# Two transformer blocks in one launch: a rearranged key-norm preparation, a recurrence whose triangular inverse runs in crossed halves with predicated copies, and a final norm inside the last stage

## The chip, the cores and the metric

One core of a Trainium2 chip runs the whole program in one launch. The metric is the device time of one execution in microseconds (us). A time is given as the median of several executions; a profiled execution is a run of its own, with its own time.

## The reference

The program computes two blocks, one after the other, on 256 tokens of width 1024, all in float32.

First block: a layer norm, then a projection `h @ w_in` that feeds two groups. One is latent attention with 8 heads. The other is a recurrence (RWKV-7) with 8 heads of 64 x 64 state. Then an output projection, a layer norm, 32 experts of which each token takes 4, and a second layer norm. The modulation vectors come from `ada_w` (1024 x 6144), which the program reads in three thirds. The recurrence, cut to its core, with the normalised key `kk`:

```
kk = k_h * k_k;  kk = kk / max(norm(kk), 1e-12)
k_h = k_h * (1 + (a_h - 1) * k_a)
sa    = state @ (-kk_t)
state = state * w_t + sa (x) (kk_t * a_t) + v_t (x) k_t
out_t = state @ r_t
o = (groupnorm(out) * gn_g + gn_b + bonus) * g
```

Second block: two layers, each a feed-forward net of width 2816, a mixing part with three kinds of attention, and a second feed-forward net; then the final norm:

```
return x * rsqrt(mean(x * x) + 1e-6) * final_norm
```

## The kernel before, in words

**Form.** Every engine has its own list of instructions, and semaphores order them across engines. The program is cut into stages (`Stage`); between two stages there is a barrier of all engines, in the profile a wait for `L221`. The activations are kept with features on partitions (`xT`, `hT`: 128 x 8 x 256). Within a stage the order is written out by hand.

**Weights.** SP issues the loads of 1 MB and 2 MB into a ring of 12 slots; a load waits until the slot's last user has told `used`. In the expert stage two rings are loaded for 32 experts, one after another. The first 8 MB for the experts are asked for in the recurrence stage (L1032 to L1035), further ones from the stage behind it and from L1486 on.

**Attention stage (L706 to L824).** TensorE goes through 8 heads: scores of head h + 2, values of head h - 1, transposes of head h (`turn`), and in `aside(h)` one unit of the second third of the modulation sums (`sum_ada`, L291). VectorE does mask, maximum, scaling; ACT the exponentials and copies. At the end ACT takes the root of the key norms (L799) and copies the modulation rows (L801).

**Preparation stage (L858 to L984).** SP loads the constants (`rc`, L870), the first output rows and eight units of `ada_w`. VectorE takes maximum and reciprocal of the key norm (L951, L952) and then a masked running sum of the decays (L957, `tensor_tensor_scan`), whose mask `no_start` comes with the constants. Behind it are the factors alpha, beta, kappa, rho (L970 to L976). TensorE spreads the key norm, makes gate, bonus and the transposes of the factors, which ACT copies to `nat`.

**Recurrence stage (L993 to L1335).** The 256 tokens are 4 chunks of 64. There are 16 systems (head half, head pair, token half) with two chunks each, one on partitions 0 to 63 and one on 64 to 127. For each the inverse of a unit lower triangular 64 x 64 matrix is grown by doubling blocks, in 5 levels (`LEVELS`, L1086). A level has, for two groups q of 8 systems: POOL masks the level's part out of the lower matrix (L1044); TensorE multiplies it with the transposed inverse (x, L1096); ACT copies the result (L1233); TensorE makes the growth of the transposed inverse (L1064) and of the inverse (L1071); VectorE adds both (L1294, L1297). Both products of a system stay on their own rows and columns of the array, so that a pair of chunks uses two of its four quarters of 64 x 64. Before the levels are the products of beta and kappa with alpha and rho (L1056) and the lower product (L1081), and VectorE's masks (L1272 to L1288). Behind them are a2v (L1113), za (L1124, L1127), ta (L1135), the chunk transition M (L1146, L1151), the inputs N (L1159, L1164), three steps over the chunks with the last third of the modulation sums between them, and the outputs.

A float32 matmul is executed in two passes. The profile has a record for each pass, and one for its weight load.

**Last stages.** The feed-forward nets split each weight into two parts of fewer bits and do three passes (`L2243`, `L2258`), with VectorE and ACT making the parts. Behind the last one VectorE adds the sums to `xT` (L2221). The final norm is a stage of its own (L2951 to L2995): squares of all columns, one sum over partitions by a product with ones (L2962), root, reciprocal, eight scalings (L2987), 16 transposes (L2968), four copies (L2979) and four stores.

## Time and profile before

| what | value |
|---|---|
| median of 3 runs | 2345.15 us |
| lowest and highest | 2336.08 and 2348.59 us |
| the profiled execution, its own time | 2340.77 us |
| its span in the profile | 2339.0 us |
| its mean granted TensorE clock | 0.974 |
| TensorE busy | 2184.0 us, 93% |
| VectorE busy | 1086.6 us, 46% |
| ACT busy | 698.2 us, 30% |
| POOL busy | 16.9 us, 1% |
| DMA | 626.63 MB, mean 268 GB/s |

A busy share is an average over stages with different limits, so the table alone does not say what bounds a stage. A row of the timeline has the start in us, the duration in us, engine and line, what is written and what is read, how many instructions are merged, and in brackets how long the engine had been idle and who ended it. A row of the windows has the stretch, its length, and for each engine the busy time and the number of instructions, then the granted TensorE clock as a share of 2.4 GHz, the mean share of the DMA engines and what they moved in GB/s.

### The profile page before, as it was taken

What the parts mean: (1) busy time and instruction counts of PE and PEld (TensorE: products, weight loads), DVE (VectorE), ACT (ScalarE), POOL (GpSimd) and SP (SyncE); (2) the same over time, 40 slices, a digit from 0 to 9 for tenths busy, and PEclk for the clock granted to TensorE, in tenths of its full rate; (3) what the DMA queues carried; (4) which work ended last, traced back from release to release, by engine and by line L of the source; (5) the groups of instructions that cost most, each with busy time, mean ns of one, the idle gap of its engine ahead of it and who ended that gap; (6) DMA issues with size and microseconds to landing.
All of it is one profiled execution on the core that took longest, in us unless ns stands there. A gap on an engine that the chain in (4) does not pass through costs nothing. (4 is left out here: it accounts for less than half of the span.)

```text
span 2339.0 us, 37294 instructions
## 1 busy us (share of the span) xinstructions
PE 2184.0 (93%) x15721; PEld 1593.4 (68%) x15721; DVE 1086.6 (46%) x1686; ACT 698.2 (30%) x884; POOL 16.9 (1%) x16
## 2 busy tenths in 40 slices
PE   6979799999999999999989999999999999999998
PEld 5757544433333333333439999879999999889997
DVE  4774511211111111111127557777566556777554
ACT  3542311111111111111115335345334334445332
POOL 0011000000000000000000000000000000000000
PEclk8989999999999999999989999999999999999999
DMA  9343789999999999999966564325555655434651
GB/s 379 138 178 148 285 344 430 430 430 430 430 430 430 430 430 430 430 430 430 414 248 198 180 192 150 109 91 193 186 181 162 198 187 173 126 100 135 199 182 52
DMA packets 200079, 626.63 MB, mean 268 GB/s; under 512 B 13160, under 2 KB 149928, under 8 KB 164136
## 3 DMA queue, kind: packets, MB, share of 16 engines
q1 hardware_dynamic: 197368, 623.41, 69.0%
q10 hardware_dynamic: 2608, 1.72, 0.3%
q8 instruction: 80, 1.31, 0.2%
q14 instruction: 23, 0.19, 0.0%
HBM read 624.05 MB, written 1.05 MB: 267 GB/s over the span
## 5 line engine op out<-in xcount | busy, mean ns | idle before, releaser
L2009 DVE TENSOR_TENSOR w_low<-ring,w_high 128x2048 fp32r<-128x2048 f32 x168 | 383.9, 2290 | 265.7 <-ACT w_high L2004 265.7
L2004 ACT ACTIVATE w_high<-ring 128x2048 fp32r<-128x2048 f32 x168 | 319.9, 1909 | 273.3 <-PE bank L2243 140.8
L1762 PE MATMUL bank<-ring,ut 128*64 128x512 f32 x1024 | 244.3, 624 | 40.6 <-DMA ring<-in_exp_w_dram 40.5
L1734 PE MATMUL bank<-ring,xt 128*64 128x512 f32 x1024 | 223.3, 594 | 0.3 <-ACT xt L1816 0.3
L1734 PE MATMUL bank<-ring_odd,xt 128*64 128x512 f32 x1024 | 223.3, 594 | 0.0
L1762 PEld LDWEIGHTS bank<-ring,ut 128*64 128x64 f32 x1024 | 71.2, 142 | 198.0 <-issue 123.2
L2258 PE MATMUL bank<-h_high,w_high 128*128 128x256 f32 x1408 | 187.3, 281 | 6.5 <-ACT h_high L2149 3.6
L2258 PE MATMUL bank<-h_high,w_low 128*128 128x256 f32 x1408 | 186.2, 281 | 1.4 <-DVE w_low L2009 1.4
L2258 PE MATMUL bank<-h_low,w_high 128*128 128x256 f32 x1408 | 186.1, 281 | 1.3 <-DVE h_low L2188 1.3
L1820 ACT ACTIVATE sg<-glu 128x512 f32<-128x512 f32 x32 | 20.2, 630 | 542.6 <-DVE glu L1883 542.6
L2258 PEld LDWEIGHTS bank<-h_high,w_high 128*128 128x128 f32 x1408 | 176.1, 189 | 7.6 <-ACT h_high L2149 4.3
L2258 PEld LDWEIGHTS bank<-h_high,w_low 128*128 128x128 f32 x1408 | 175.4, 189 | 1.7 <-DVE w_low L2009 1.7
L2258 PEld LDWEIGHTS bank<-h_low,w_high 128*128 128x128 f32 x1408 | 175.3, 189 | 1.5 <-DVE h_low L2188 1.5
L1899 DVE SCALAR_TENSOR_TENSOR xT<-bank,mod,xT 128x256 f32<-128x256 f32 x128 | 55.6, 480 | 247.4 <-PE bank L1776 247.4
L1734 PEld LDWEIGHTS bank<-ring,xt 128*64 128x64 f32 x1024 | 72.3, 137 | 143.1 <-issue 143.1
L1734 PEld LDWEIGHTS bank<-ring_odd,xt 128*64 128x64 f32 x1024 | 72.2, 137 | 142.9 <-issue 142.9
L1882 DVE TENSOR_SCALAR lin<-bank 128x256 f32<-128x256 f32 x64 | 26.7, 417 | 257.6 <-PE bank L1734 257.6
L1875 DVE TENSOR_SCALAR choose<-base 128x128 fp32r<-128x128 f32 x32 | 9.1, 287 | 236.0 <-PE bank L1762 236.0
L1833 ACT ACTIVATE y<-bank 64x512 f32<-64x512 f32 x64 | 37.9, 592 | 259.5 <-PE bank L1762 258.7
L2243 PE MATMUL bank<-u_high,w_low 128*128 128x256 f32 x704 | 92.0, 279 | 0.0
L2243 PE MATMUL bank<-u_low,w_high 128*128 128x256 f32 x704 | 91.9, 279 | 0.0
L2243 PE MATMUL bank<-u_high,w_high 128*128 128x256 f32 x704 | 91.9, 279 | 0.0
(544 smaller groups left out, 2813.4 us busy)
## 6 DMA issues: line engine op xcount, KB each, us to landing
ring<-in_exp_w_dram SPq DMA_DIRECT2D x64, 2048.0 KB, 27.2
ring_odd<-in_exp_w_dram SPq DMA_DIRECT2D x64, 2048.0 KB, 28.4
ring<-in_exp_w_dram SPq DMA_DIRECT2D x128, 1024.0 KB, 25.6
ring<-in_ffn_w_gate_dram SPq DMA_DIRECT2D x44, 1024.0 KB, 5.4
ring<-in_ffn_w_up_dram SPq DMA_DIRECT2D x44, 1024.0 KB, 5.4
ring<-in_ffn_w_down_dram SPq DMA_DIRECT2D x44, 1024.0 KB, 4.9
ring<-in_w_in_dram SPq DMA_DIRECT2D x36, 1024.0 KB, 5.4
ring<-in_ada_w_dram SPq DMA_DIRECT2D x24, 1024.0 KB, 12.7
```

Of the source, the lines that this page charges most:

```text
L1734: ins = nc.tensor.matmul(bank[b][at:at + SLOTS, :], xt[:, c, SLOTS * side:SLOTS * side + SLOTS], (ring, ring_odd)[side][:, c, 512 * q:512 ...
L1762: ins = nc.tensor.matmul(bank[2 + dh][64 * dh:64 * dh + 64, :], ut[:, r % 4, 64 * (r // 4):64 * (r // 4) + 64], w[:, x, 512 * dh:512 * dh ...
L1820: nc.scalar.activation(sg[:, :], glu[:, :], ACT.Sigmoid, scale=SW_ALPHA).then_inc(sem("sg_ready"), 1)
L1833: nc.scalar.activation(y[64 * side:64 * side + 64, 512 * dh:512 * dh + 512], bank[2 + dh][64 * dh:64 * dh + 64, :], ACT.Copy).then_inc(sem ...
L1875: nc.vector.tensor_scalar(choose[:, side, :], const("half_of"), const("expert_of")[:, bass.ds(e, 1)], None, ALU.mult).then_inc(sem("chosen ...
L1882: nc.vector.tensor_scalar(lin[:, 256 * b:256 * b + 256], pairs[:, :, 1], LIMIT, -LIMIT, ALU.min, ALU.max)
L1899: ins = nc.vector.scalar_tensor_tensor(xT[:, m, :], bank[6 + n % 2][:, T * j:T * j + T], mod[:, 40 + m:41 + m], xT[:, m, :], ALU.mult, ALU ...
L2004: nc.scalar.activation(w_bufs[0][u % BUFS], ring2[:, u % RING2, :], ACT.Copy).then_inc(high2, 1)
L2009: nc.vector.tensor_tensor(w_bufs[1][u % BUFS], ring2[:, u % RING2, :], w_bufs[0][u % BUFS].bitcast(F32), ALU.subtract).then_inc(low2, 1)
L2243: ins = nc.tensor.matmul(sums(m // 2)[:, T * (m % 2):T * (m % 2) + T], w[:, at:at + P], v[:, T * x:T * x + T], start=(g == 0 and k == 0 an ...
L2258: ins = nc.tensor.matmul(b[:, T * x:T * x + T], w[:, at:at + P], h[:, c, :], start=(k == 0 and x == 0 and c == 0), stop=(k == 2 and c == D ...
```

## The change

In words, stage by stage:

- **Attention.** The eight units of modulation sums are added two at a time in `aside` of heads 0 to 3. The root of the key norm is taken behind the exponentials of the last head; maximum, reciprocal and the copy of the modulation rows go to VectorE, ahead of its last copy. ACT ends with a sigmoid of one column.
- **Preparation.** `no_start` is made with two memsets. The copies of `gate` on ACT go behind the exponentials. The transposes of the modulation rows go to another bank and right behind the key product. A second table, the block masks (12 x 64 bytes a partition), is loaded; the table of constants shrinks from 1728 to 192 columns.
- **Recurrence.** ACT sets `inv` and `inv_t` to the identity and copies the lower product unmasked. VectorE puts the first blocks in by `copy_predicated` with byte masks. The lower product is made a second time with its two factors' places on the rows crossed. The systems are in two groups, even and odd; the rows of the inverse of the even ones are exchanged. Growth of the transposed inverse of one group is put in turn with x of the other group. Each growth is put in by `copy_predicated` from a bank. POOL has no work. `a2v` lies beside `nat` (which grows by a fifth), and za is one product of 128 columns. ACT's clears go between its copies, VectorE's bonus and gate scaling behind za. The second load of output rows waits for `n_ready`.
- **Last stage.** The final norm is part of the last feed-forward stage. Transposes are products of `xT` with a diagonal of the gains; row sums are products of the squares with one column of ones; root and reciprocal are on two columns; the factor comes in with the last copies, half on ACT and half on VectorE.

The core of the diff:

```diff
@@ attention
-                    sum_ada(pe, 1, bank[6], range(h, h + 1))
+                    if h < 4:
+                        sum_ada(pe, 1, bank[6], range(2 * h, 2 * h + 2))
...
+                def key_inverse():
+                    dve.wait_ge(sem("key_root"), 1)
+                    st.step(nc.vector.tensor_scalar(key_norm, key_norm, 1e-12, None, ALU.max))
+                    nc.vector.reciprocal(key_norm, key_norm)
+                    dve.wait_ge(used, UNIT[("ada1", ADA_THIRD - 1)] + 1)
+                    nc.vector.tensor_copy(mod_rows[:, :], bank[6][:, :])
@@ preparation
-                dve.wait_ge(sem("const_loaded"), 16)
+                st.step(nc.vector.memset(no_start, 1.0))
+                st.step(nc.vector.memset(no_start[:, 0:HP * T:CH], 0.0))
                 dve.wait_ge(sem("acts_done"), 1)
...
                 dve.wait_ge(sem("factor_ready"), 1)
                 st.step(nc.vector.tensor_tensor(flat(k), flat(k), factor, ALU.mult))
+                dve.wait_ge(sem("mod_turned"), 1)
@@ recurrence
-                sp.wait_ge(sem("ta_ready"), 1)
+                sp.wait_ge(sem("n_ready"), 1)
                 load_unit(sp, "wo", 0, wo_rows(1), 2)
...
+            def inverse_rows(s_, ph):
+                return half_rows(ph if s_ % 2 else 1 - ph)
...
+                for n in range(LEVELS):
+                    wait_x(n, 1)
+                    wait_growth_t(n, 0)
+                    for s_ in range(0, NS, 2):
+                        for ph in range(2):
+                            grown = growth_t(s_, ph)
+                        for ph in range(2):
+                            ins = x_product(s_ + 1, ph)
+                    grown.then_inc(sem("growth_t0"), 1)
+                    ins.then_inc(sem("x_ready1"), 1)
+                    growth(n, 0)
+                    if n in KAPPA_LEVELS:
+                        pe.wait_ge(sem("products_taken"), 4 + 2 * n)
+                        products(kappa, n, lambda h2: 6 + h2)
...
-                            nc.tensor.matmul(bank[s_ // 4][r, at:at + 64], inv_t[r, s_, :], nat[r, 0, a, head_cols(h2, hp)], start=True, stop=True)
-                        for ph in range(2):
-                            r = half_rows(ph)
-                            ins = nc.tensor.matmul(bank[s_ // 4][r, at + 64:at + P], inv_t[r, s_, :], a2v[r, s_, :], start=True, stop=True)
+                            ins = nc.tensor.matmul(bank[s_ // 4][r, at:at + P], inv_t[r, s_, :], nat[r, 0:5:4, a, head_cols(h2, hp)], start=True, stop=True)
...
+                        st.tell(nc.vector.copy_predicated(group(inv_t, g), block_mask(6 + n + 1, 8), bank[2 + g][:, :].rearrange("p (s t) -> p s t", t=CH)),
+                                f"grown_t{g}")
@@ last stage
+                turn(0)
+                turn(1)
+                pe.wait_ge(sem(f + "squares_summed"), 2)
+                for a in range(TT):
+                    for c in range(2):
+                        nc.tensor.matmul(sums_at[:, a:a + 1], squares[:, c, P * a:P * a + P], ones[:, 0:1], start=(a == 0 and c == 0), stop=False,
+                                         skip_group_check=True)
+                pe.wait_ge(sem(f + "last_squares"), 4)
...
+                turn(2)
+                turn(3)
```

## Rows read from the trace of the kernel before

**Rows 1.** Windows, expert stage and a later layer; columns as told above
```profile
350.00:400.00 50.00, 49.89 (x246) 21.38 (x244) 11.13 (x30) 6.17 (x11) 0.00 (x0) 1.00 1.01 431
1350.00:1400.00 50.00, 50.00 (x427) 50.00 (x426) 29.67 (x24) 18.62 (x12) 0.00 (x0) 1.00 0.59 189
```

**Rows 2.** Timeline of the last 20 us; columns as told above
```profile
2318.37 0.63 PE L2243 MATMUL bank<-u_low,w_high 128*128 128x256 f32 x4
2319.04 0.69 DVE L2221 SCALAR_TENSOR_TENSOR xT<-bank,xT 128x512 f32<-128x512 f32 x1 [0.72 <-PE bank L2243]
...
2321.94 6.68 PE L2962 MATMUL bank<-ring,base 128*128 128x256 f32 x16 [2.94 <-ACT ring L2974]
...
2334.81 1.10 ACT L2979 ACTIVATE ring<-bank 128x512 f32<-128x512 f32 x2 [0.26 <-PE bank L2968]
```

**Rows 3.** Timeline of the preparation stage
```profile
142.70 2.29 DVE L957 TENSOR_TENSOR_SCAN ring<-rwkv_const,ring 128x1024 f32<-128x1024 f32 x1 [3.72 <-DMA rwkv_const<-in_const_rwkv_dram]
...
155.48 1.60 ACT L946 ACTIVATE nat<-bank 128x512 f32<-128x512 f32 x3
```

**Rows 4.** Timeline of the recurrence: levels, and the first za product
```profile
165.28 1.64 DVE L1283 TENSOR_TENSOR ring<-ring,rwkv_const 128x512 f32<-128x512 f32 x1
...
182.21 2.04 PE L1096 MATMUL bank<-ring 64*64 64x64 f32 x64
...
187.81 2.05 PE L1096 MATMUL bank<-ring 64*64 64x64 f32 x64
...
188.82 3.70 DVE L1302 SCALAR_TENSOR_TENSOR bonus<-bonus,params,gate 128x256 f32<-128x256 f32 x4
...
199.57 0.33 PE L1124 MATMUL bank<-nat,ring 64*64 64x64 f32 x4
```

**Rows 5.** Timeline, TensorE: products on four quarters, and passes with 128x128 weights
```profile
157.88 1.98 PE L1056 MATMUL bank<-alpha_rho,beta 64*64 64x128 f32 x64 [1.70 <-PEq L221]
...
159.65 1.14 PE L1081 MATMUL bank<-beta,alpha_rho 64*64 64x64 f32 x64
160.58 1.08 PE L1056 MATMUL bank<-alpha_rho,ps 64*64 64x128 f32 x31
...
224.67 3.79 PE L1194 MATMUL bank<-alpha_rho,states 128*128 128x64 f32 x32
```

**Rows 6.** Timeline, TensorE: first products behind a stall named issue
```profile
163.67 0.27 PE L1056 MATMUL bank<-alpha_rho,ps 64*64 64x128 f32 x1 [2.02 <-issue]
...
207.61 0.27 PE L1146 MATMUL bank<-nat,ring 64*64 64x64 f32 x2 [1.82 <-issue]
...
211.35 0.27 PE L1159 MATMUL bank<-ring,nat 64*64 64x64 f32 x2 [1.64 <-issue]
```

**Rows 7.** Windows, and the instruction queue's packets from 165 to 200 us
```profile
165.00:200.00 35.00, 33.45 (x1007) 33.06 (x1009) 27.01 (x37) 6.81 (x12) 11.90 (x9) 0.87 0.02 4
207.60:209.80 2.20, 2.10 (x128) 1.96 (x128) 0.00 (x0) 1.14 (x4) 0.00 (x0) 1.00 0.62 240
...
q8 instruction: 8, 0.13, 1.6%
```

**Rows 8.** Timeline of the attention stage and of its end
```profile
114.67 0.55 PE L609 MATMUL bank<-base,probs 128*128 128x128 f32 x3 [0.93 <-DVE probs L653]
115.15 1.06 PE L291 MATMUL bank<-ring,c_wide 128*32 128x512 f32 x8
...
135.17 0.42 DVE L658 COPY hT<-bank 128x256 f32<-128x256 f32 x1 [3.45 <-PE bank L618]
...
136.81 1.28 ACT L922 ACT_TABLE_LOAD   x1 [0.75 <-PEq L221]
```

**Rows 9.** Source line of a predicated copy in the second block: min, median, max ns
```profile
L2793 DVE COPY_PREDICATED hT<-level_masks,bank x64: 429/436/453, 1472.0 to 2084.9; 128x256 f32<-128x256 uint8 x64
```

**Rows 10.** Windows of 1 us with the granted clock
```profile
147.00:148.00 1.00, 0.00 (x0) 0.00 (x0) 0.96 (x2) 1.00 (x2) 0.00 (x0) 0.50 1.05 442
164.00:165.00 1.00, 0.00 (x0) 0.00 (x0) 1.00 (x1) 0.00 (x0) 1.00 (x2) 0.50 0.00 0
```

More of the change, by code:

```diff
@@ L935, in _ @@
                 st.tell(ins, "factor_ready")
-                act.wait_ge(sem("gate_ready"), 1)
-                for j in range(2):
-                    ins = nc.scalar.activation(flat(gate[:, 2 * j:2 * j + 2, :]), bank[4 + j][:, :], ACT.Copy)
-                st.tell(ins, "gate_taken")
                 act.wait_ge(sem("csum_ready"), 1)
@@ L942, in _ @@
                 st.tell(nc.scalar.activation(e2, csum, ACT.Exp, scale=EXP_M05), "exps")
+                act.wait_ge(sem("gate_ready"), 1)
+                for j in range(2):
+                    nc.scalar.activation(flat(gate[:, 2 * j:2 * j + 2, :]), bank[4 + j][:, :], ACT.Copy)
                 for n in range(8):
@@ L1107, in _, with place, x_product, growth_t @@
-                pe.wait_ge(sem("products_taken"), 8)
-                for q in range(2):
+                def place(b, rows, s_):
+                    return bank[b][rows, CH * (s_ // 2):CH * (s_ // 2) + CH]
+                def x_product(s_, ph):
+                    return nc.tensor.matmul(place(4 + s_ % 2, inverse_rows(s_, ph), s_), low[half_rows(ph), s_, :], inv_t[half_rows(ph), s_, :],
+                                            start=True, stop=True)
+                def growth_t(s_, ph):
+                    r = inverse_rows(s_, ph)
+                    return nc.tensor.matmul(place(2 + s_ % 2, half_rows(ph), s_), inv[r, s_, :], xs[r, s_, :], start=True, stop=True)
@@ new lines, in growth @@
+                def growth(n, g):
+                    if n == LEVELS - 1:
+                        return
+                    if n == 0:
+                        pe.wait_ge(sem("products_taken"), 2)
+                    for s_ in range(g, NS, 2):
+                        for ph in range(2):
+                            r = inverse_rows(s_, ph)
+                            ins = nc.tensor.matmul(place(g, r, s_), xs[r, s_, :], inv[r, s_, :], start=True, stop=True)
+                    ins.then_inc(sem(f"growth{g}"), 1)
@@ new lines, in _ @@
+                for x in (inv_t, inv):
+                    st.tell(nc.scalar.activation(x, rconst("same").unsqueeze(1).to_broadcast([P, NS, CH]), ACT.Copy), "identities")
+                act.wait_ge(sem("low_product"), 1)
+                for h2 in range(2):
+                    st.tell(nc.scalar.activation(flat(low[:, 8 * h2:8 * h2 + 8, :]), bank[4 + h2][:, :], ACT.Copy), "low_ready")
+                for n in range(LEVELS):
+                    for g in range(2):
+                        act.wait_ge(sem(f"x_ready{g}"), n + 1)
+                        st.tell(nc.scalar.activation(group(xs, g), bank[4 + g][:, :].rearrange("p (s t) -> p s t", t=CH), ACT.Copy), f"x_taken{g}")
@@ L1278, in _ @@
-                for q in range(2):
-                    st.step(nc.vector.tensor_tensor(low[:, 8 * q:8 * q + 8, :], bank[4 + q][:, :].rearrange("p (s t) -> p s t", t=CH),
-                                                    eight("below"), ALU.mult), "low_ready")
-                for q in range(2):
-                    part = slice(8 * q, 8 * q + 8)
-                    st.step(nc.vector.tensor_tensor(inv_t[:, part, :], lt[:, part, :], eight("lower1_t"), ALU.mult))
-                    st.step(nc.vector.tensor_tensor(inv_t[:, part, :], inv_t[:, part, :], eight("same"), ALU.add), "inv_ready")
@@ L2196, in ffn @@
+        def ffn(S, f, L, base_unit, norm_name, first, flip, update, after, tables=None, opens=None, closes=None):
             sem = S.sem
@@ L2368, in _ @@
                         tables[1](dve, n - (LOOP_AT + REPS * LOOP2))
-                if not after:
+                if closes:
+                    closes[3](dve, next_update)
+                elif not after:
                     for m in range(4):
```

382 lines of the change are left out of this document (214 added, 168 removed).

## The prediction

> **What bounds the kernel now.** I read the windows first. From 350 us on the expert stage runs its DMA engines full at 431 GB/s, and the two later layers keep TensorE busy for 50 us in 50 [rows 1]. The change touches neither; both simply start when what precedes them ends. So a microsecond won before 258 us, where the experts' loads follow one another, or behind the last matmul of the last layer, is won once and whole. That leaves three stretches: attention and preparation (95 to 157 us), recurrence (157.9 to 231 us) and the tail.
>
> **Tail.** Its timeline is a pure chain. The last update of xT ends at 2319.73; a stage barrier, squares, sixteen passes of the ones product (6.68 us), root, reciprocal, scalings, transposes and copies follow; the last copy ends at 2335.91 and the span 3.1 us later [rows 2].
>
> **Preparation.** VectorE waits 3.72 us, until 142.70, for the recurrence's constants; then it is busy for 14.2 us, and ACT's last copy ends at 157.08 [rows 3]. VectorE's chain sets this stage.
>
> **Recurrence.** A level has three products of 64 records each (32 matmuls in two passes) and takes 5.6 us: x starts at 182.21 and at 187.81, with no gap on TensorE [rows 4]. 5.6/192 is 29 ns a record. Where neighbouring matmuls use all four quarters of the array, 64 records take 0.93 us (159.65 to 160.58), 14.5 ns each [rows 5]. But such runs end in stalls in which nothing is waited for that the profile shows ("issue"): 1.82 us before 207.61 and 1.64 us before 211.35, their ends 3.74 us apart, and an earlier one of 2.02 us before 163.67, beside heavy loads [rows 6]. Between the two later ones TensorE has exactly 128 matmul and 128 weight-load records; and from 165 to 200 us its 2016 records come with 8 packets of the instruction queue, 252 a packet [rows 7]. I read this as code that arrives in pieces of 128 matmuls, each usable about 3.7 us after the piece before it begins. The earliest stall says the same: 128 records before 161.66 is about 158.8, so 4.9 us under loads. At 29 ns a piece lasts 3.74 us: today its arrival just hides.
>
> **Part 1: attention and preparation.** (a) The eight modulation sums go from one a head to two a head over the first four heads. One costs TensorE about 1.0 us; it idles 0.93 us before the next turn and as much before the one after, which takes up two of them [rows 8]. The others shift 1 us each from late heads to early ones, and the softmax chain of the late heads gives it back only in part. I take 0.2 us gained. (b) The root of the key norms, with its table load, moves under head 5; maximum, reciprocal and the copy of mod_rows (2.7 us) go to VectorE ahead of the last pair's copy, where it idles 3.45 us [rows 8]; the sigmoid's table load, 1.28 us from 136.81, is paid in the stage before [rows 8]. The sigmoids start about 0.5 us sooner. (c) The scan's mask comes from two memsets, 1.2 us in a place where VectorE waits for the sigmoids (which end near 139.7) anyway; so the scan starts at about 139.1, not 142.70. (d) Behind it stand the same 14.2 us, but with new waits: for factor_ready (about 0.2, its ACT chain now being the later) and for mod_turned (about 0.5, behind the gate products on TensorE); rk, TensorE's bonus product and all factors queue behind these. (e) The mask load issues in 0.4 us on SP, ahead of wo_first and the ada loads, which nobody awaits before 212 us. The stage ends at about 154.4 instead of 157.08: **-2.7 us**, between -1.5 and -3.9.
>
> **Part 2: recurrence.** Removed: POOL's masks, beside which a VectorE operation of 128x512 took 1.64 us, not 0.69 [rows 2, 4], and the masks before the first x. Added: a second lower product, 64 records. Four predicated copies a level replace four additions; the nearest row is one from a bank, 128x256 in 0.436 us [rows 9], so I take 0.70 for 128x512, between that row's 0.44 (if size costs nothing) and 1.4 (if strided groups cost double). 2.8 us a level lie under TensorE.
>
> Crossed, growth_t of one group and x of the other share a block on four quarters, 0.93 us for 64 records; growth alone stays on two, 0.93 for 32. A level is 4 x 0.93 = 3.74 us, with the hand-overs to ACT and VectorE 4.0. But its 192 records are 1.5 pieces of code, 1.5 x 3.74 = 5.6 us, as today. From the stage's start to the first za product stand 64+128+64+896+64 = 1216 records. If the stage starts at 155.2, record 159 waits for code until 161.0 (4.9 us under loads), the next piece until 164.9, and (1216-159-128)/128 = 7.3 pieces of 3.74 end near 192. Today za starts at 199.57 [rows 4]: 7.6 sooner, of which 2.7 is Part 1, so **-5.0**. Joint products: za has 64 records of 128 columns instead of 128 of 64. Columns set the time (64 records of 64x128 take 1.77 us, of 64x64 0.93 [rows 5]), so its 3.7 us stay: 0, at best -1.8. The idle from 158.3 to 161.0 may halve the clock: TensorE idled from 145.3 and from 161.7, and the clock read 0.50 at 147 and at 164 [rows 10]. A piece at half clock takes 5.0 us instead of 3.74; one and a half of them cost 2 us, at even odds 1.0. **The stage: -4.0**, between +1 and -14.
>
> Moved out of the levels: bonus (at most 3.70 us on VectorE [rows 4]) and gate scaling (less), now behind za's copies. Queued behind them are the additions of squares, awaited on TensorE only behind M and N. On today's times they would be done near 210, while N still runs after 211.35 [rows 6], so nothing; uncovered it would be some 4.8. ACT's clears go between copies at 0.34 each, hidden by the code's arrival. The second wo load waits for n_ready instead of ta_ready, some 7.6 us longer; behind it on SP stand four 2 MB loads that wait for modulation sums behind N in any case; they land some 2.5 us later (1 MB at the full rate of [rows 1]), before the experts need them.
>
> **Part 3: tail.** Turns 0 and 1 are 16 passes; with 128x128 weights a pass takes 0.12 us (32 in 3.79 [rows 5]). They follow the last matmul, 2319.0, at once: 2320.9. The additions of squares end at 2320.4, hidden. Sixteen one-column passes at 0.12 give the row sums by 2322.8; root and reciprocal of two columns add 0.6; turns 2 and 3 end at 2324.8, the last scaled copies (0.7) at 2325.5. The stores' 3.1 us, and 0.2 as the last two leave together: 2328.8. **-10.2 us**, between -8 and -11.5. The eight gain activations, 2.3 us, lie on ACT behind its last weight split, beside matmuls.
>
> **Sum.** -2.7 - 4.0 - 10.2 = -16.9 us on the profiled execution's 2340.77: 2323.9. The median shown is 2345.15, all four executions average 2342.65; I add this 1.9: **2325.8**.
>
> **Rivals.** (A) *The code arrives in time.* Levels run at 4.0, two with 0.9 for kappa; za starts near 182, Part 2 is -14, all -27: 2315.7. For it: no stall stands within the levels of today; against it, those of [rows 6]. Chance 0.22. The Trainium skill, "Runtime: NRT & Kernel Launch", section "Instruction fetch mechanics", says that instruction memory is refilled in blocks of 256 instructions and that crossing a block is mostly hidden. By that rule A would hold. The count of 256 agrees with [rows 7]; the stalls don't agree with the hiding.
> (B) *The recurrence gains nothing*, because pieces take 4.2 us throughout (nine cost 4 more) or the low clock lasts three pieces: -13, 2329.7. Chance 0.20.
> (C) *The crossing doesn't overlap*, two operand groups not sharing the array: 5.6 us a level without stalls. -15.5, 2327. Chance 0.06.
> (D) *Slower: predicated copies.* If one over strided groups with a byte mask takes c us, VectorE sets a level at 4c + 0.3. That decides from c = 1.3; at 2.2 the 17 us are gone, at 2.9, four times the row's price, the kernel is at 2357. [Rows 9] speak against it. Chance 0.03.
> (E) *The tail keeps half*, one-column passes being dearer or the clock falling among them: -12, 2330.7. Chance 0.07.
> The forecast keeps 0.42.
>
> **How the numbers follow.** The cases reach from 2315.7 to 2330.7. The runs of before spread over 12 us, so a median can stand 3 off: range 2313 to 2334. A difference of 0.5%, 11.7 us, is about what a measurement of this kernel tells from none. Faster by more than that: all of A (0.22), 0.39 of the forecast, 0.05 of C, 0.16 of B and E: 0.82. Slower: D, 0.03. The rest 0.15.
>
> **What would show it.** The mask scan should start near 139. TensorE's waits should list six or more "issue" stalls of 1 to 2 us between 155 and 195, za should start near 192, predicated copies take 0.7, POOL have nothing in the stage, and the last copy end 5.8 us after the last update. If a level takes 4 us without such stalls, my reading of the code's arrival is wrong and A holds; if predicated copies take over 1.3 us, D does.

## The result, and the profile after

| | before | changed |
|---|---|---|
| median | 2343.8 us (7 runs) | 2327.8 us (7 runs) |
| lowest, highest | 2336.08, 2348.59 | 2324.49, 2329.43 |
| profiled execution, its span | 2340.77, 2339.0 | 2324.49, 2322.7 |
| mean granted clock | 0.974 | 0.975 |

The ratio is 0.9934, interval 0.9918 to 0.995. The forecast was 2325.8 in a range of 2313 to 2334, and it lies 2.0 us off. The traces show that two of its terms were wrong in opposite directions.

The first table gives the start of the same step in both profiled executions, in us from the start of the span. Each is the first start that the trace has for the source line.

| step | before | changed | stretch to it, before | changed | forecast |
|---|---|---|---|---|---|
| preparation, first product | 136.84 | 138.70 | 136.8 | 138.7 | Part 1 (a): -0.2 |
| scan of the decays | 142.70 | 143.43 | 5.9 | 4.7 | |
| recurrence, first product | 157.88 | 161.06 | 15.2 | 17.6 | Part 1: -2.7 |
| first product for za | 199.57 | 196.46 | 41.7 | 35.4 | -5.0, +1.0 for the clock |
| squares of the outputs summed | 212.19 | 207.68 | 12.6 | 11.2 | 0 |
| mixing stage, first sum | 232.57 | 228.09 | 20.4 | 20.4 | 0 |
| last update of xT | 2319.04 | 2312.66 | 2086.5 | 2084.6 | 0 |
| end of the span | 2339.0 | 2322.7 | 20.0 | 10.0 | Part 3: -10.2 |

Part 1 came out at **+3.2** instead of -2.7, Part 2 at **-7.7** instead of -4.0, Part 3 at -9.9; the middle gave -1.9. They make the 16.3 us between the spans. ("Mixing stage" here and below is the stage right behind the recurrence, in which the outputs are normalised and projected.)

Windows of the changed kernel; the first two answer to [rows 1], the last to the first of [rows 7]:

```profile
350.00:400.00 50.00, 49.89 (x246) 21.37 (x244) 11.14 (x30) 6.17 (x11) 0.00 (x0) 1.00 1.00 428
1350.00:1400.00 50.00, 50.00 (x427) 50.00 (x426) 28.73 (x25) 18.80 (x12) 0.00 (x0) 1.00 0.56 182
...
165.00:196.00 31.00, 25.32 (x1098) 24.09 (x1092) 18.30 (x30) 10.19 (x20) 0.00 (x0) 1.00 0.02 4
```

The two far stages are as before. In the recurrence POOL is idle, and TensorE gets through 1098 matmul records in 31 us where it had 1007 in 35.

Timeline of the changed kernel's attention end and preparation, for [rows 3, 8]. The doubled sums are the 16 records of L288:

```profile
119.46 0.55 PE L608 MATMUL bank<-base,probs 128*128 128x128 f32 x3 [0.18 <-DVE probs L652]
119.94 1.92 PE L288 MATMUL bank<-ring,c_wide 128*32 128x512 f32 x16
...
123.44 0.55 PE L608 MATMUL bank<-base,probs 128*128 128x128 f32 x3
...
133.58 0.65 PE L616 MATMUL bank<-turned,v_nat 128*64 128x256 f32 x2 [1.77 <-ACT turned L692]
...
138.70 2.47 PE L894 MATMUL bank<-ps,w_kv 64*128 64x256 f32 x5 [1.28 <-PEq L218]
...
144.25 3.78 PE L900 MATMUL bank<-ring 128*128 128x256 f32 x8
```

```profile
131.47 1.28 ACT L802 ACT_TABLE_LOAD   x1
...
143.43 2.29 DVE L969 TENSOR_TENSOR_SCAN ring<-alpha_rho,ring 128x1024 f32<-128x1024 f32 x1 [3.32 <-ACT ring L936]
...
148.07 1.66 DVE L972 SCALAR_TENSOR_TENSOR ring<-ps,params,bank 128x256 f32<-128x256 f32 x4 [2.35 <-PE bank L900]
```

A head with two sums takes 3.98 us from turn to turn (119.46 to 123.44), and TensorE is full in it. Late heads no longer have a sum, so TensorE idles: 1.77 us ahead of 133.58, while ACT loads the root's table. The last turn starts 1.6 us later than before. Then comes what I had not forecast. These windows of the changed kernel have the granted clock as the third number from the end:

```profile
134.00:135.00 1.00, 1.00 (x7) 0.64 (x4) 1.00 (x1) 0.00 (x0) 0.00 (x0) 0.65 0.00 0
135.00:147.00 12.00, 10.14 (x29) 7.14 (x28) 4.70 (x8) 6.92 (x15) 0.00 (x0) 0.50 0.60 212
```

Before, the clock was full here until TensorE idled from 145 us on. Now all of the preparation's first products run at half clock. VectorE's scan waits for the sigmoids that follow from them, and then 2.35 us more for the key norm's spread (L900, 3.78 us).

The recurrence, for [rows 4, 6]: the first products, two of the stalls, and the list of TensorE's waits (in us: total, number, longest).

```profile
161.06 1.52 PE L1062 MATMUL bank<-alpha_rho,beta 64*64 64x128 f32 x32 [2.09 <-PEq L218]
...
173.12 0.27 PE L1070 MATMUL bank<-ring 64*64 64x64 f32 x2 [0.39 <-issue]
...
176.97 0.27 PE L1099 MATMUL bank<-ring 64*64 64x64 f32 x2 [0.76 <-issue]
```

```profile
PE bank L1099 <- issue: 2.0, 3, 0.8
PE bank L1075 <- issue: 1.6, 2, 1.0
PE bank L1209 <- issue: 1.4, 1, 1.4
PE bank L1196 <- issue: 1.0, 1, 1.0
...
PE bank L1070 <- issue: 0.4, 1, 0.4
```

Six stalls named issue within the levels, 4.0 us, and two more behind za. Between these stalls TensorE waited twice for another engine, 0.9 and 0.8 us. Predicated copies of 128x512, for [rows 9]:

```profile
L1354 DVE COPY_PREDICATED ring<-block_masks,bank x10: 710/731/734, 169.8 to 195.6; 128x512 f32<-128x512 uint8 x10
```

The tail, for [rows 2]:

```profile
2312.46 1.95 PE L2275 MATMUL bank<-prods,xT 128*128 128x128 f32 x16
2312.66 0.69 DVE L2373 SCALAR_TENSOR_TENSOR xT<-bank,xT 128x512 f32<-128x512 f32 x1
...
2318.02 0.75 DVE L2332 TENSOR_SCALAR ring<-bank,r_tok 128x512 f32<-128x512 f32 x1 [0.74 <-PE bank L2275]
```

Between the last update and the last scaled copy 16.2 us had passed; now it is 5.4 (2313.35 to 2318.77), with TensorE transposing while the row sums' inputs are made.

### The profile page after: what moved, and what is told of

Its sections match the earlier page's. It is cut to its first block and busy times, and to the rows that moved or that the text cites. A ratio compares the mean times of both kernels' runs of the same rounds, so it can differ in the third digit from the quotient of the medians.

```text
span 2322.7 us, 37284 instructions
## 1 busy us (share of the span) xinstructions
PE 2178.0 (94%) x15737; PEld 1584.7 (68%) x15737; DVE 1075.6 (46%) x1681; ACT 704.4 (30%) x897; POOL 3.0 (0%) x6
## 5 line engine op out<-in xcount | busy, mean ns | idle before, releaser
L1896 ACT ACTIVATE y<-bank 64x512 f32<-64x512 f32 x64 | 37.9, 593 | 258.4 <-PE bank L1825 257.6
```

Source lines behind the costliest of these rows:

```text
L1896: nc.scalar.activation(y[64 * side:64 * side + 64, 512 * dh:512 * dh + 512], bank[2 + dh][64 * dh:64 * dh + 64, :], ACT.Copy).then_inc(sem ...
```

## The experiments

Eleven more runs were made, in three groups; one of them is the changed kernel itself again. The kernels of a group share the runs of the kernel before, whose median was 2339.23, 2339.91 and 2340.09 us in them. In the comparison above it was 2343.8, so medians are set against each other only within a group, and across groups by their ratio to before. Three questions were open: why Part 1 lost instead of winning, whether the arrival of code sets the levels, and whether the tail's gain stands alone.

### What went wrong ahead of the recurrence

Two parts of the attention's change were undone, alone and together. **sums_spread** takes the doubled sums back:

```diff
-                    if h < 4:
-                        sum_ada(pe, 1, bank[6], range(2 * h, 2 * h + 2))
+                    sum_ada(pe, 1, bank[6], range(h, h + 1))
```

> The changed kernel with one unit of modulation sums a head again, over all eight heads; all else as changed. Theory 1 (the root of the key norms and its table load, ahead of the copy that head 6 waits for, cost the 2 us and drop TensorE's clock): the recurrence's first product stays within 1 us of 161.06 us, the clock still falls near 134 us, total 2327. Rival (two sums a head delay the late heads): the first product comes at 158 or sooner and the total is 3 us lower, 2324.

**root_back** takes root, inverse and the copy of mod_rows back to where they were:

```diff
-                att_act(act, st, S, take_others, key_root)
-                nc.scalar.activation(kk_squares[:, 0:1], ones[:, 0:1], ACT.Sigmoid)
+                att_act(act, st, S, take_others, lambda: None)
+                key_root()
+                act.wait_ge(used, UNIT[("ada1", ADA_THIRD - 1)] + 1)
+                nc.scalar.activation(mod_rows[:, :], bank[6][:, :], ACT.Copy)
...
+                st.step(nc.vector.tensor_scalar(key_norm, key_norm, 1e-12, None, ALU.max))
+                st.tell(nc.vector.reciprocal(key_norm, key_norm), "norm_inverted")
```

> The changed kernel with the root of the key norms back behind the last head on ACT, the copy of mod_rows there too, and maximum and reciprocal back at the start of preparation on VectorE; two sums a head stay. Theory 1: TensorE no longer idles 1.8 us twice near 133, so the clock stays at full through preparation; preparation starts near 137.5 and the recurrence's first product is at 156 to 157.5, 4 to 5 us before the changed kernel's 161.06; total 2323. Rival (two sums a head are the cost): first product at 160 or later, total 2327.

**both_back** is the two edits together.

> Both of these undone; preparation keeps its memsets and the early mod_turned. Theory 1: the attention stage ends as before the change, preparation starts at 136.8, the mask scan at 139.8 instead of 142.70, and the recurrence's first product at 155 to 156; total 2322. Rival (the scan's start does not set the stage): 157.5 or later, total 2324 or more.

Measured, with the starts in each profiled execution:

| | median (runs) | ratio to before | preparation | scan | recurrence | za |
|---|---|---|---|---|---|---|
| changed | 2327.8 (7) | 0.9934 [0.9918, 0.995] | 138.7 | 143.4 | 161.1 | 196.5 |
| sums_spread | 2321.16 (4) | 0.993 [0.991, 0.995] | 135.8 | 138.7 | 153.8 | 191.3 |
| root_back | 2331.35 (5) | 0.9958 [0.9941, 0.9975] | 137.0 | 141.4 | 159.9 | 196.5 |
| both_back | 2325.79 (4) | 0.9937 [0.9921, 0.9954] | 137.4 | 141.5 | 158.6 | 195.7 |

The intervals of the ratios overlap, so here the marks decide, not the medians. With the sums spread, the recurrence starts 7.3 us sooner, as the rival in that run's expectation had it. The scan stands 2.9 us behind the first preparation product (138.7 from 135.8), where it was 5.9 before the change and 4.7 in the changed kernel; the clock is full. Undoing the root's move instead gives only 1.2 us, where theory 1 had 4 to 5: TensorE still idles in the late heads, and its clock still falls. So my first suspect, the root's table load alone, falls.

But the doubled sums alone are not the cause either. both_back has neither, and missed its expectation (155 to 156 us) by some 3 us: its clock is full through the heads and falls behind the stage boundary. Timeline of sums_spread:

```profile
135.77 1.31 PE L893 MATMUL bank<-ps,w_kv 64*128 64x256 f32 x5 [1.28 <-PEq L218]
```

of both_back:

```profile
137.35 1.92 PE L895 MATMUL bank<-ps,w_kv 64*128 64x256 f32 x5 [1.71 <-PEq L218]
```

and of the kernel before:

```profile
136.84 1.31 PE L879 MATMUL bank<-ps,w_kv 64*128 64x256 f32 x5 [1.71 <-PEq L221]
```

In both_back, as before the change, TensorE stands still for 1.71 us at the boundary, because ACT still loads the root's table and copies; in sums_spread for 1.28. The clock was 0.50 from 138 to 144 us in both_back. Yet in the kernel before it stayed at 1.00 until 146 us, behind the same idle time and the same products. So this fall is not explained by the idle time alone, and what decides it stays open. What it costs is clear: from the first preparation product to the recurrence's first it is 18.1 us in sums_spread at full clock, 21.2 in both_back, 22.4 in the changed kernel and 22.8 in root_back.

That left two causes in one: do the doubled sums cost by their place in the heads, or by the clock that falls on the idle time they leave? **filled_gaps** keeps them and adds eight products that nobody reads:

```diff
+                    if h > 5:
+                        for _ in range(2 if h != 6 else 6):
+                            nc.tensor.matmul(bank[0][:, 0:T], ident, w_uv[:, 0:T], start=True, stop=True)
```

> The changed kernel with eight products added that nobody reads (identity times 256 columns of w_uv, into bank 0, no longer in use there): six behind the transposes of head 6 and two behind those of head 7, where TensorE idles 1.77 and 0.58 us. Two sums a head stay. In the changed kernel the granted clock falls to 0.50 at 134 us and stays so until 147 us; the first preparation product starts at 138.70 us, the recurrence's first product at 161.1 us. With one sum a head again (the run sums_spread) these are 135.8 and 153.8 us at full clock. Theory that the idle time behind the doubled sums costs twice, by the heads' period and by the clock that falls upon it: with the gaps filled the clock stays at 1.00 until the stage boundary at least, the key norm's spread comes sooner, and the recurrence starts 2 to 5 us sooner (156 to 159 us), the attention's end within 1 us of 138.7. Rival, that the clock falls for other reasons (the wait at the stage boundary, the low activity of the narrow products) or that the preparation isn't bound by TensorE: the recurrence still starts at 160.5 us or later.

Beside it ran sums_spread and the changed kernel once more, without an edit.

> The same kernel as sums_spread, beside the changed kernel on one chip. By the traces the stretch up to 223 to 228 us is 5.1 us shorter than in the changed kernel. Theory that this is the kernel's and not an execution's: the recurrence starts 5 to 8 us sooner than in changed_again, and the median is 3 to 6 us below it. Rival, that the difference lies within what executions of one kernel vary by: the marks differ by less than 2 us, the medians too.

> The changed kernel itself once more, for comparison with the other two on one chip. Its medians so far: 2327.8 us; first preparation product 138.7 us, recurrence's first product 161.1 us, first product for za 196.5 us, granted clock 0.50 from 135 to 147 us. If these are the kernel's own, they come within 0.5 us again and the clock's fall with them; if the clock's fall was one execution's, the recurrence starts near 157 us.

| | median (runs) | lowest, highest | ratio to before | preparation | recurrence | za | mixing |
|---|---|---|---|---|---|---|---|
| filled_gaps | 2321.26 (4) | 2319.79, 2322.83 | 0.9917 [0.9896, 0.9938] | 137.7 | 155.6 | 193.5 | 224.1 |
| sums_spread_again | 2325.07 (6) | 2321.76, 2327.63 | 0.9933 [0.9915, 0.995] | 137.4 | 155.4 | 193.0 | 224.7 |
| changed_again | 2328.71 (6) | 2322.0, 2331.17 | 0.9948 [0.9929, 0.9967] | 138.6 | 160.5 | 196.3 | 228.3 |

Windows of filled_gaps:

```profile
127.00:134.00 7.00, 6.42 (x35) 4.44 (x33) 5.75 (x18) 4.88 (x13) 0.00 (x0) 1.00 0.01 2
135.00:147.00 12.00, 9.29 (x51) 7.32 (x49) 7.88 (x16) 9.79 (x18) 0.00 (x0) 1.00 0.69 259
```

and of changed_again:

```profile
127.00:134.00 7.00, 4.65 (x25) 2.75 (x23) 5.73 (x19) 4.88 (x13) 0.00 (x0) 0.93 0.00 0
135.00:147.00 12.00, 10.14 (x28) 7.29 (x28) 4.04 (x7) 7.03 (x15) 0.00 (x0) 0.51 0.60 212
```

The clock's fall repeats with the kernel: all five traces that have the changed kernel's attention (the changed kernel twice, uncrossed, odd_x_left_out, one_column_added) show 0.50 or 0.51 from 135 to 147 us. The three with the sums spread and the root moved show 0.97 to 1.00. Filling the idle time takes the fall away. Eight useless products (2.76 and 1.03 us on TensorE) bring the recurrence forward by 4.9 us against changed_again. At 155.6 us it starts 0.4 us ahead of the expected 156 to 159. Three of filled_gaps' four runs lie below all of changed_again's, and its median is 7.4 us lower, though the intervals of the two ratios still touch. Of that, 4.2 us stand in the marks at the mixing stage. The rest is not in the traces: behind that mark the profiled execution of filled_gaps took 3.5 us more than that of changed_again (2086.9 and 2083.4), so their spans differ by 0.7 us only. Executions of one kernel differ by as much there (see below).

Of the 4.9 us, 4.0 lie in the preparation, which takes 17.9 us in place of 21.9; its first product comes 0.9 us sooner. So the cost of the doubled sums is the clock. Their longer heads cost next to nothing by themselves: filled_gaps still has them, and starts the recurrence at 155.6, sums_spread_again at 155.4. Spread sums fill the same gaps with work that is needed. sums_spread's first trace had the preparation at 135.8, its second at 137.4, so 1.6 us of the first comparison belonged to the execution. Against the second trace both_back's recurrence starts 3.2 us later, not 4.8. sums_spread_again starts it 5.1 us ahead of changed_again; its median is 3.6 lower. Both are as its theory expected.

### Does the arrival of code set the levels?

**uncrossed** leaves the rows of the even systems unexchanged, so that growth_t and x no longer share the four quarters:

```diff
-                return half_rows(ph if s_ % 2 else 1 - ph)
+                return half_rows(ph)
```

> The changed kernel with the rows of the even systems' inverse not exchanged, so that growth_t of one group and x of the other share two quarters of the array; same number of records. Theory (code arrives in pieces of 128 matmul records in 3.7 us): no more issue stalls between 172 and 195, since 29 ns a record is what the pieces allow, and from the recurrence's first product to za's first the time is 35.4 us, as in the changed kernel, within 1.5 us. Rival (four quarters shorten a level): a level takes 1.9 us more, five levels 8 to 9 us, so 44 us and a total of 2336.

Measured 2328.75 us (4 runs), ratio 0.9955 [0.9939, 0.9972]. From the recurrence's first product to za it is 36.7 us (160.8 to 197.5), 1.3 more than in the changed kernel's first trace and 0.9 more than in its second (35.9). That is within the 1.5 us of the theory and far from the rival's 44. Windows of the changed kernel, 22 us within the levels and two short ones in them:

```profile
171.00:193.00 22.00, 17.79 (x808) 16.92 (x799) 13.12 (x20) 7.01 (x15) 0.00 (x0) 1.00 0.02 4
...
184.00:186.00 2.00, 2.00 (x103) 1.91 (x96) 0.94 (x3) 0.93 (x2) 0.00 (x0) 1.00 0.04 8
186.00:188.00 2.00, 1.00 (x64) 0.87 (x55) 0.62 (x1) 0.08 (x1) 0.00 (x0) 1.00 0.00 0
```

and of uncrossed:

```profile
171.00:193.00 22.00, 22.00 (x757) 21.98 (x753) 12.62 (x20) 6.95 (x14) 0.00 (x0) 1.00 0.02 4
...
184.00:186.00 2.00, 2.00 (x72) 1.98 (x69) 0.75 (x2) 0.39 (x1) 0.00 (x0) 1.00 0.03 8
186.00:188.00 2.00, 2.00 (x76) 2.00 (x73) 1.47 (x2) 1.01 (x2) 0.00 (x0) 1.00 0.00 0
```

(The short windows count a record twice where it crosses their edge.) Crossed, TensorE runs through 103 matmul records in 2 us, then stands idle for half of the next 2 us. Uncrossed it is never idle and makes 72 to 76. Over the 22 us that is 808 records against 757. The crossing makes the bursts faster, and the waits take nearly all of it back. The fairest pair is uncrossed and changed_again, whose first stall, in the crossed lower product, ends at 165.74 and 165.72 us: crossed reaches za 1.2 us sooner. Rival A, with all levels at the burst's rate, would have had it some 10 us sooner.

That the stalls are the ends of pieces can be counted. These windows reach from the end of one stall to the end of the next, two of the changed kernel, then two of one_column_added (below), where other products stand at these places:

```profile
173.12:176.97 3.85, 3.10 (x128) 2.94 (x127) 2.91 (x5) 1.91 (x4) 0.00 (x0) 1.00 0.02 4
176.97:180.56 3.59, 2.95 (x128) 2.87 (x128) 1.46 (x2) 1.01 (x2) 0.00 (x0) 1.00 0.02 5
```

```profile
187.33:191.44 4.11, 3.02 (x129) 2.93 (x129) 1.47 (x2) 1.01 (x2) 0.00 (x0) 1.00 0.01 4
191.44:195.54 4.10, 2.98 (x128) 2.85 (x127) 1.47 (x2) 1.01 (x2) 0.00 (x0) 1.00 0.01 4
```

Each time it is 128 matmul records and as many weight loads, give or take one, in 3.6 to 4.1 us. And the count goes by the list of instructions, not by the products: filled_gaps adds 8 products, that is 16 matmul records, far ahead in the attention stage, and there the first stall of the recurrence comes 16 records sooner. First changed_again, then filled_gaps:

```profile
163.18 0.67 PE L1108 MATMUL bank<-beta,alpha_rho 64*64 64x64 f32 x31
165.72 0.70 PE L1108 MATMUL bank<-beta,alpha_rho 64*64 64x64 f32 x33 [1.88 <-issue]
```

```profile
158.28 0.43 PE L1111 MATMUL bank<-beta,alpha_rho 64*64 64x64 f32 x15
161.57 0.93 PE L1111 MATMUL bank<-beta,alpha_rho 64*64 64x64 f32 x49 [2.86 <-issue]
```

No wait for data would move so.

**odd_x_left_out** leaves out 15 of the 16 products x of the odd group in each of the five levels, so that its inverse is no longer the right one; **one_column_added** puts a product of one column ahead of every growth_t:

```diff
-                        for ph in range(2):
-                            ins = x_product(s_ + 1, ph)
+                        if s_ == NS - 2:
+                            ins = x_product(s_ + 1, 1)
```

```diff
+                    nc.tensor.matmul(place(2 + s_ % 2, half_rows(ph), s_)[:, 0:1], inv[r, s_, :], xs[r, s_, 0:1], start=True, stop=True)
```

> Leaves out the products x of the next level for all but one (15 of 16 a level for the 5 levels after the first, some 75 products and 75 weight loads): the powers' products and growth stay, with their copies and their waits; the values of the odd group are not the reference's. The stretch from the recurrence's first product to the first for za is 35.4 us in the changed kernel, and its instruction queue lands a piece of 256 records every 3.7 us there. Theory that code arrival sets the stretch: 150 records fewer are 150 x 14.5 ns = 2.2 us by 3.7 us for 256 records, so the stretch falls by about 2.2 us, and by up to 4.4 us where half of the records' time is the products' own streaming at 29 ns. Rival, that the chain of copies and products from level to level sets it (the group left out is off that chain): it stays within 0.7 us.

> Adds a product of one column, written over at once by the product behind it, before every growth product, with its weight load: 16 a level over 5 to 6 levels, some 80 to 96 products and as many loads, 160 to 190 records. The stretch from the recurrence's first product to the first for za is 35.4 us in the changed kernel. Theory that code arrival sets the stretch: 160 to 190 records x 14.5 ns = 2.3 to 2.8 us longer, about 37.9 us. Rival, that streaming or the copies between levels set it: a weight load and a one-column product take no more than the time of a load that overlaps, and the levels have idle time behind their copies, so it stays within 0.8 us.

Both expectations count badly, and the trace corrects them. A float32 product is two passes, each a matmul record and a weight-load record, so it is four records. And growth_t is issued for both groups. The source line of the added product has 320 matmul records and as many loads, 640 in all:

```profile
L1075 PEld LDWEIGHTS bank<-ring x320: 129/135/135, 168.2 to 204.9; 64*64 64x64 f32 x160
L1075 PE MATMUL bank<-ring x320: 160/193/214, 168.3 to 204.9; 64*64 64x1 f32 x160
```

At the prediction's 3.74 us for 256 records 640 are 9.3 us. Measured: the stretch grew by **10.2 us**, from 35.4 to 45.6 (160.5 to 206.1). Each of the two kernels ran once; this one took 2334.5 us. In odd_x_left_out 75 products are 300 records or 4.4 us by that rate; measured: **3.2 us** less (161.2 to 193.4). That lies between the recorded bounds of 2.2 and 4.4, and the rival's 0.7 is out. The 3.2 us are net of a stall of 0.9 us ahead of the levels that the changed kernel's first trace lacks; from the first growth to za it is 4.2 us less (169.6 to 193.4 against 168.5 to 196.5). In its levels only one stall named issue is left, of 0.5 us: with fewer records the code is nearly in time. The instruction queue's packets between 165 us and za, in the order changed, uncrossed, odd_x_left_out, one_column_added:

```profile
q8 instruction: 8, 0.13, 1.7%
```

```profile
q8 instruction: 8, 0.13, 1.7%
```

```profile
q8 instruction: 7, 0.11, 1.6%
```

```profile
q8 instruction: 11, 0.18, 1.8%
```

They are 8 in 31 us, 8 in 32, 7 in 28 and 11 in 41: a packet every 3.7 to 4.0 us, whatever the products do. The spacing alone proves little, since uncrossed takes its records at that rate without a stall. But in one_column_added every piece from 173 us to za still ends in a stall named issue (0.2 to 1.1 us), so there the code, and not the added products' own time, comes last.

**spread_and_wide** tried to make use of this behind za. It has the sums spread, and adds the identity to M by 4 products of 512 columns, not 64 of 64:

```diff
+                for h2 in range(2):
+                    for ph in range(2):
+                        r = half_rows(ph)
+                        nc.tensor.matmul(bank[6 + ph][half_rows(h2), :].rearrange("p (s j) -> p s j", j=64), ident[r, r],
+                                         ident[r, None, r].to_broadcast([64, 8, 64]), start=True, stop=False, skip_group_check=True)
...
-                                ins = nc.tensor.matmul(bank[6 + ph][half_rows(h2), at:at + 64], ident[r, r], ident[r, r], start=False, stop=True)
```

> The changed kernel with two edits at once: one sum a head in the attention (as in the run sums_spread, which took 2321.2 us), and the identity added to M by 4 products of 512 columns in place of 64 products of 64. The stretch from the first product for za to the sum of squares of the outputs is 11.2 us in the changed kernel, and its products with 64 columns stand 29 ns apart or less, apart from the stalls for code (1.4 and 1.0 us there). Theory that the stretch from za on is bound by TensorE's records: 60 products and 60 weight loads fewer, 60 x 29 ns = 1.7 us, less 4 x 0.21 us for the wide ones = 0.9 us gained at least, and with 120 records of code fewer up to half a stall more (0.7 us): 0.9 to 1.6 us, so 2319.6 to 2320.3 us. Rival, that ScalarE's and VectorE's copies behind za set this stretch: nothing gained, 2321.2 us. With the sums spread, the preparation's first product starts near 136 us at the full granted clock (in the changed kernel 138.7 us at 0.50).

From za to the squares' sum it is 8.9 us (192.0 to 200.9) against 11.2 in sums_spread, 2.4 less, and two stalls there shrink to one of 0.3. The expectation had 0.9 to 1.6. (Its 1.7 us for the records took a matmul record for a product; 60 products are 240 records, 3.5 us by the code's rate.) But the median is 2324.89 us (5 runs), ratio 0.9933 [0.9918, 0.9948], no better than sums_spread. In its trace za started 0.7 us later than in sums_spread, and 0.8 us more were lost between the squares' sum and the mixing stage, which starts 0.8 us sooner (222.1 and 223.0). That stage's first four passes take 3.27 us instead of 1.96: the clock again. From there to the last update its execution took 2090.6 us, against 2084.8. Whether the edit helps the whole kernel stays open.

### The tail alone

**tail_alone** is the kernel before with the closing only: the final norm inside the last feed-forward stage, nothing else changed.

```diff
+                closes = closing(S, "z_", flip ^ 4) if L == LAYERS - 1 else None
...
-                     flip ^ 4, update, False)
+                     flip ^ 4, update, False, closes=closes)
```

> The kernel before with the closing alone: the final norm's tables, gains and the transposed halves of the output beside the last product, everything ahead of it as before. Theory that the parts add up and the closing is worth the 9.9 us read from the traces: 2339.2 - 9.9 = 2329.3 us, with 10.1 us from the last product's end to the end of the span. Rival, that the closing also slows the last products (its gains and its table load lie beside them): less than 9 us gained, and the stretch from the last gather to the last product longer than in the kernel before by over 1 us.

Measured 2330.12 us (5 runs), ratio 0.9961 [0.9943, 0.9979]: 9.8 us less than the kernel before beside it, where 9.9 were expected. Its last update and last copy in the timeline:

```profile
2318.22 0.69 DVE L2310 SCALAR_TENSOR_TENSOR xT<-bank,xT 128x512 f32<-128x512 f32 x1
...
2323.58 0.75 DVE L2269 TENSOR_SCALAR ring<-bank,r_tok 128x512 f32<-128x512 f32 x1 [0.74 <-PE bank L2212]
```

From the end of the one to the end of the other it is 5.4 us as in the changed kernel, and the span ends 10.1 us after the last update's start. The stretch from the mixing stage to that update, 2085.3 us (from 232.9), is not longer than in the kernel before (2086.5), so no cost of the gains and the table load beside the last products shows.

## Why the prediction was right in sum and wrong in its parts

**What bounds the kernel: right.** The stages between the mixing stage's first sum and the last update took 2083.4 to 2091.1 us in all thirteen traces, whatever had been won ahead of them.

**Part 1, step (a): the step that failed.** I took 0.2 us gained for the doubled sums; the preparation's first product came 1.9 us later and the recurrence's 3.2. My argument was that the late heads' softmax chain gives the moved microsecond back only in part. I priced TensorE's time in the heads and never asked what TensorE would do in the heads that lost their sum. It idles there, and its clock falls to 0.50 for 12 us, over the very products on which ACT and VectorE wait. [Rows 10] had shown me two such falls behind idle time, and I used them for the recurrence alone. The runs put a price on it: with the gaps filled, the recurrence starts 4.9 us sooner. Steps (a) and (b) also worked on each other: the 1.77 us of idle time is a late head without its sum and with (b)'s table load.

**Part 1, steps (b) to (d): right, under a full clock.** I had the scan 2.3 us behind the first preparation product (139.1 and 136.84) and the recurrence at 155.2. With the sums spread it is 2.9 to 3.0 us, and the recurrence starts at 153.8 and 155.4.

**Part 2: the mechanism was right, a size was off.** From the first product to za I had 36.8 us (155.2 to 192); the changed kernel took 35.4 and 35.9 in its two traces, and the other runs that keep its recurrence 36.6 to 37.9. The stalls are there, in the number forecast (six in the levels), though shorter: 0.4 to 1.0 us, not 1 to 2. The long one that I had put at 2.7 us, early in the stage beside full loads, stands where I had it, behind 159 matmul records. In sums_spread it ends 6.1 us after the recurrence's first product, where I had 5.8:

```profile
159.91 1.14 PE L1107 MATMUL bank<-beta,alpha_rho 64*64 64x64 f32 x33 [2.69 <-issue]
```

In the first trace of the changed kernel it is missing: the clock was 0.50 from 162 to 165 us, and the records themselves took the time. In changed_again, at full clock, it is there with 1.9 us, and the first products x start 5.8 us after the stage's first product (166.24), in the other trace 5.4 us (166.47). With the recurrence starting at 153.9 to 159.9 us the stall ends 5.8 to 6.1 us later, at 160.5 only 5.2 us later. So a late start is in part made good: of the 5.1 us between changed_again and sums_spread_again 3.3 are left at za.

The 3.7 us by which Part 2 came out better are three sizes: 1.3 in the stretch to za, 1.4 in the stretch from za to the squares' sum, which I had at nothing (-1.8 at best for the joint products), and 1.0 for the clock. No run separates the joint products from the bonus and scaling moved there. As for the clock, sums_spread_again has it at 0.50 from 163 to 169 us and takes 9.1 us for the 317 matmul records behind its first growth, where sums_spread takes 7.9. Yet they reach za 37.6 and 37.5 us after their first product, as the stalls behind are shorter. So the piece at half clock was no invention, but the stage paid nothing for it in the end.

Rival A (code in time, za 10 us sooner) did not come, nor did D, by which predicated copies bind: 0.73 us against 0.70 taken and 1.3 needed. Against B speak pieces of 3.6 to 3.9 us, not 4.2; against C the 103 records in 2 us; against E the tail's -9.9.

The Trainium skill, "Runtime: NRT & Kernel Launch", section "Instruction fetch mechanics", says that crossing a block of 256 instructions is mostly hidden. These traces don't agree: within the levels alone 4.0 us of stalls stand at such crossings, and taking 300 records out or putting 640 in moved the stage by 3.2 and 10.2 us.

**Part 3: right.** 5.8 us from last update to last copy were forecast, 5.4 measured; -10.2 against -9.9 in the profile and -9.8 in the medians of tail_alone.

**The total** is near the median because +5.9 of Part 1 met -3.7 of Part 2 and -1.9 in the middle, which the sum had at nothing. That middle can't be told from chance: from the mixing stage to the last update the traces have 2083.4 (changed_again), 2084.6 (changed), 2084.8 (sums_spread), 2086.5 (before), 2089.0 (sums_spread_again), 2090.6 (spread_and_wide) and 2091.1 us (root_back). Up to 7.7 us of one execution's time lie in stages whose products no edit touched, 4.2 us between two executions of one kernel. The 1.9 us that I added for the profiled execution against the median is of this kind; in the changed kernel it was 3.3. That the sum came within 2.0 us of the median is luck as much as mechanism.

**A version better than both** is one without Part 1's doubled sums. Beside the changed kernel in one group, sums_spread_again has a median 3.6 us lower and reaches the mixing stage 3.6 us sooner; filled_gaps has 7.4 and 4.2. The intervals of all three ratios touch, so the marks carry this, and between the two no run decides. In the first group the ratio of sums_spread is 0.993 against the changed kernel's 0.9934, no difference that counts. I would keep sums_spread, which does no useless work.

## What to carry over

Before moving work off a tensor engine's list, look at what remains in the place it leaves: idle time there can halve the clock of the next stage, which costs more than the moved instructions did. When matmuls are small, count four records for each float32 product and compare them with the rate at which instruction packets land (here 256 records in some 3.7 us); beyond that rate, clever packing of the array buys bursts and stalls, and only fewer instructions buy time. When a sum of parts meets the total, still check each part at its own mark in the trace.

## What was not expected of the hardware

- All four quarters of the array in use hardly sped up this stream of 64x64 products: 808 against 757 matmul records in 22 us, crossed and uncrossed. Each burst was faster, but nearly each piece of 256 records ended in a wait for the next.
- Sixteen matmul records added in one stage moved a stall two stages later by exactly 16 records.
- Eight products whose results nobody reads, 3.8 us of TensorE time, brought the recurrence forward by 4.9 us, and the median was 7.4 us lower: the granted clock stayed at 1.00, not 0.51, from 135 to 147 us.
- Whether the clock falls at a stage boundary hangs on little. With TensorE idle for 1.28 us it stayed at 1.00 (sums_spread); with 1.71 us it was 0.50 soon after in both_back, and stayed at 1.00 in the kernel before and in tail_alone. What decides is not settled by these runs.
- A predicated copy of 128x512 from a bank with a byte mask takes 0.73 us, the same as the scaled copy of 128x512 in the tail (0.75).
